# Five more norms summed in rows, and the pooling weights' low part on GpSimd instead of VectorE

## The chip, the cores and the metric

The kernel runs on one core of a Trainium2 chip. Its time is device microseconds of one launch. Five engines run their own instruction streams and meet at semaphores: TensorE (PE in the rows; PEld its weight loads), VectorE (DVE), ScalarE (ACT), GpSimd (POOL) and SyncE (SP), which issues the loads of the weights. Weights and activations come from HBM into SBUF; matmuls write PSUM, eight banks.

## The reference

A prompt of 128 tokens and a latent of 1024 tokens, 1024 channels each, go through two layers. Layer 0 mixes tokens with a gated linear recurrence in both directions, layer 1 with means over windows of 2, 4, 8 and 16 tokens. After each mixer comes a SwiGLU block of width 2816. Every block has an RMS norm ahead of it and one behind it:

```python
def rms_norm(x, g):
    return x * lax.rsqrt(jnp.mean(x * x, axis=-1, keepdims=True) + EPS) * g

def layer_forward(x, cond, p, h0):
    sh1, sc1, g1, sh2, sc2, g2 = modulation(cond, p['mod_w'], p['mod_b'])
    h = rms_norm(x, p['mix_pre_g']) * (1.0 + sc1) + sh1
    y = rglru_mixer(h, ...) if p['kind'] == 'rglru' else pool_mixer(h, ...)
    x = x + g1 * rms_norm(y, p['mix_post_g'])
    h = rms_norm(x, p['ffn_pre_g']) * (1.0 + sc2) + sh2
    gate, up = jnp.split(h @ w_in, 2, axis=-1)
    return x + g2 * rms_norm((silu(gate) * up) @ w_out, p['ffn_post_g'])

def pool_mixer(h, pool_w, pool_b, pool_scale):
    pooled = [centred_window_mean(h_gi, win) - h_gi for gi, win in enumerate((2, 4, 8, 16))]
    return (einsum('btgc,gcd->btgd', pooled, pool_w) + pool_b) * pool_scale
```

## The kernel before, in words

Activations lie channels on partitions, tokens on columns. The 1152 tokens form three column groups (0, 1 and 2) of 384. Every product of float32 operands is made of three matmuls: each operand is split into a high part, rounded to the matmul's format, and a low part, the rest; high by high, low by high and high by low are added up in PSUM (line 1042). In the rows mv and hid are moving operands, w the weights, each with _hi and _lo.

**Weights.** They come in granules of 128x2048 floats (1 MB). SP loads granule q of the stream into one of two raw slots (lines 970 to 1017; line 980 is the load itself) and waits until the low part of granule q-2 is made. ACT makes the high part (`split_hi`, line 1488) into one of three weight slots; the low part, raw minus high, is made by GpSimd in one instruction (`split_lo`, line 2665), by VectorE in one (line 2210), or by VectorE in two halves (`split_lo_half`, line 2217), put between its additions of outs into y (line 2485). Which it is, `HALVES`, `AFTER_POOL`, `ON_DVE` and `ON_POOL` say.

**SwiGLU steps.** A step (layer, s) takes one block of 256 hidden channels for one or more groups: gate and up products, the hidden product on VectorE (line 2462) with its parts by ACT (line 1800) and VectorE (line 2465), then eight outs, m = 0 to 7, added into y by VectorE, or taken by ACT where they are the first (line 1808). Three steps also carry the pooling mixer's products of one group (`POOL_AFTER`): step (0, 17) has group 0's, (1, 1) group 1's, (1, 6) group 2's. Ahead of these, ACT makes the high parts of three granules: the pooling weights, then the next step's gate, then its up. In time the three lie at 1258, 1429 and 1582 us.

**Norms.** Each group has norms numbered in order; in layer 0, norm 1 is the mixer's post norm and norm 2 the SwiGLU's pre norm, both in the stage of the out projection (about 430 to 565 us). ACT squares, GpSimd adds the squares over the eight channel tiles (line 2682), TensorE adds over partitions. It does so in one of two forms. In columns: three 128x1 sums (line 1128, two matmul passes each), VectorE adds epsilon and inverts (lines 2066, 2067), ACT takes the root (line 1518), and TensorE spreads the result over the partitions (line 1139). In rows, for the norms (group, number) listed in `ROWS`: one product with a matrix of ones that leaves the sum on all partitions (line 1117), ACT's root of the whole row (line 1512), and four reciprocals of 128x96 on VectorE (line 2083).

**Order.** Each engine's order is written out when the program is built. `feed_forward_work` lists the steps' work with a place in TensorE's time, `planned` puts the norms' chains into the gaps by estimated costs (`INVERSE` is that of one reciprocal), and `upto` emits what is due. An engine runs its instructions strictly in that order.

Of the kernel before, what the change touches and what calls it, by code (L numbers as in the profile page):

```python
# [104 lines left out]
POOL_AFTER = {(0, SNAKE + 11): 0, (1, 1): 1, (1, 6): 2}  # L105
# [12 lines left out]
def own(layer, s):  # L118

    return own(layer, s - 1) if s and STEPS[layer][s - 1][0] == STEPS[layer][s][0] else s  # L120
# [34 lines left out]
WEIGHT = {item: w for w, item in enumerate(i for i in STREAM if i[0] != "mod")}  # L155
# [156 lines left out]
def norm_cols(g, n):  # L312
    return UNEVEN[g] if n in UNEVEN_NORMS else EVEN[g]
# [71 lines left out]
def places(t):  # L385

    return [t + k / KT * AT_PRODUCT["gate"] for k in PLACES]
# [6 lines left out]
def next_granules(layer, s):  # L394

    if last_own(layer, s) != s:
        return []
    later = [WEIGHT[i] for i in STREAM[Q["down", layer, own(layer, s)] + 1:] if i[0] != "mod"]
    return later[:3 if (layer, s) in POOL_AFTER else 2]


SPLIT_HI, SPLIT_LO, SMALL, TAKE, FOLD = 2.0, 4.6, 0.3, 1.2, 1.0
FIRST_DVE, FIRST_MARGIN, BESIDE_POOL, LATE = 0.5, 1.0, 0.35, 1.0
OP = {"DVE": 0.7, "ACT": 0.6, "POOL": 1.1}
MOD_SUM, COEFS, SUM, ROOT, SPREAD, TURN_Y, LANDING, PE_MARGIN = 7.7, 4.0, 1.5, 1.7, 1.2, 1.2, 9.0, 1.5
INVERSES, INVERSE = 4, 0.6
ROWS = [(0, 3), (0, 4), (0, 5), (0, 7), (1, 1), (1, 3), (1, 4), (1, 5), (1, 6), (1, 7), (2, 3), (2, 4), (2, 5), (2, 6)]


def feed_forward_work():  # L410


    work, hooks = [], []
    for i, n in enumerate(W_OUTS):
        hooks += places(AT_WOUT[i])
        work.append(("ACT", ("take", n), AT["out", n], TAKE))
    for w, t in J1_SPLITS.items():
        low = ("DVE", 2.2) if w in DVE_SPLITS else ("POOL", SPLIT_LO)
        work += [("ACT", ("split", w), t, SPLIT_HI), (low[0], ("split", w), t + SPLIT_HI, low[1])]
    for g, t in ((1, MIXED_T[0]), (2, MIXED_T[1])):  # L420
        for part, (t0, t1) in enumerate(MIXED_PARTS):
            work += [("ACT", ("mixed", g, part), t + part * 1e-3, 0.45 * (t1 - t0)),
                     ("DVE", ("mixed", g, part), t + 0.5 + part * 1e-3, 0.5 * (t1 - t0))]
    for layer in range(2):
        for s in range(len(STEPS[layer])):
            groups = STEPS[layer][s][1]
            t = AT["gate", PAIR[layer, s, groups[0], 0]] - AT_PRODUCT["gate"]
            if own(layer, s) == s:
                w = WEIGHT["down", layer, s]
                t += DOWN_LATER if (layer, s) == (0, 0) else 0.0  # L430
                low = ("DVE", 2.2) if w in LAST_SPLITS else ("POOL", SPLIT_LO)
                work += [("ACT", ("split", w), t, SPLIT_HI), (low[0], ("split", w), t + SPLIT_HI, low[1])]
            if (layer, s) == (0, 1):
                work.append(("DVE", ("mod", -1), AT["gate", PAIR[layer, s, groups[0], 0]] + 0.4, MOD_SUM))
            for g in groups:
                for j in range(HB):
                    k = PAIR[layer, s, g, j]
                    t = AT["up", k]
                    for at in (AT["gate", k] - AT_PRODUCT["gate"], AT["gate", k]):
                        hooks += places(at) if at < FIRST_END or at >= LAST_BEGIN else [at]  # L440
                    one = FIRST_DVE if not FIRST_END <= t < LAST_BEGIN else OP["DVE"]
                    work += [("ACT", ("silu", k), AT["gate", k], OP["ACT"]), ("DVE", ("mul", k), t, one),
                             ("ACT", ("hi", k), t + 0.8, OP["ACT"]), ("DVE", ("lo", k), t + 1.6, one)]
                    if k in SUM_AFTER_PAIR:
                        work.append(("DVE", ("mod", k), t + 2.4, MOD_SUM))
                    if k in (COEFS_AFTER, LAST_COEFS_AFTER):
                        work.append(("DVE", ("coefs", k), t + 2.4, COEFS))
            for w in next_granules(layer, s):
                i = next_granules(layer, s).index(w)
                at = LATE_UP if w in AFTER_POOL else 1.5 + SPLIT_HI * i  # L450
                work.append(("ACT", ("split", w), t + at, SPLIT_HI))
                if w in HALVES:
                    for half, (g, m) in enumerate(HALVES[w]):
                        work.append(("DVE", ("split", w, half), AT["out", OUT[layer, s, g, m]] + 0.75, 1.1))
                elif w in AFTER_POOL:
                    work.append(("DVE", ("split", w), t + at + SPLIT_HI, 2.2))
                else:
                    before = [v for v in next_granules(layer, s)[:i] if v in ON_POOL]
                    at = 9.0 if (layer, s) in POOL_AFTER else 1.5 + SPLIT_HI + SPLIT_LO * len(before)
                    work.append(("POOL", ("split", w), t + at, SPLIT_LO))  # L460
            outs = [(n, True) for g in groups for n in range(OUT[layer, s, g, 0], OUT[layer, s, g, KT - 1] + 1)]
            if (layer, s) in POOL_AFTER:
                outs += [(OUT["pool", POOL_AFTER[layer, s], m], False) for m in range(KT)]
            for i, (n, added) in enumerate(outs):
                if not 0 < i < 4 or AT["out", n] >= LAST_BEGIN:
                    hooks.append(AT["out", n] - AT_PRODUCT["out"])
                if n in FRESH:
                    work.append(("ACT", ("add", n), AT["out", n], OP["ACT"]))
                elif added:
                    work.append(("DVE", ("add", n), AT["out", n], FIRST_DVE if not FIRST_END <= AT["out", n] < LAST_BEGIN else OP["DVE"]))  # L470
    return work, hooks


def planned():
# [31 lines left out]
    def norm(chain, g, squared):  # L506
# [5 lines left out]
        summed = put(("PE", chain, g), added, SUM)  # L512
        if (g, norms[g] - 1) in ROWS:
            t = put(("ACT", chain, g), summed, ROOT)
# [157 lines left out]
def halves():  # L672


    places, late = {}, []
    for layer in range(2):
        for s, (b, groups) in enumerate(STEPS[layer]):
            later = next_granules(layer, s)
            if (layer, s) in POOL_AFTER:
                places[later[0]] = [(groups[-1], 3), (groups[-1], 4)]  # L680
                late.append(later[2])
            elif later and later[0] in LAST_SPLITS:
                for w, g in zip(later, groups):
                    places[w] = [(g, 3), (g, 5)]
            elif later and len(groups) == 1 and (layer, s) != (0, 0):
                places[later[1]] = [(groups[-1], 5), (groups[-1], 7)]
    return places, late
# [8 lines left out]
def program(nc, a, scratch_x, scratch_h, consts, outs):  # L696
    ctx = ExitStack()
    at = [(nc.sbuf_base + 31) // 32 * 32]
# [72 lines left out]
    with ctx:  # L771
# [110 lines left out]
        def ready(w):  # L882

            return (w_lo_dve, ON_DVE.index(w) + 1) if w in ON_DVE else (w_lo_pool, ON_POOL.index(w) + 1)
# [17 lines left out]
        def spread_count(g, n):  # L902
            return sum((g, v) not in ROWS for v in range(n + 1))

        def spread_of(g, n):

            t0, t1 = norm_cols(g, n)
            return bank[norm_bank(g, n)][:, SPREAD_AT:SPREAD_AT + t1 - t0]
# [119 lines left out]
        def _(pe):  # L1028
# [74 lines left out]
            def norm_sum(g):  # L1103
# [11 lines left out]
                t0, t1 = norm_cols(g, n)  # L1115
                if (g, n) in ROWS:
                    pe.matmul(spread_of(g, n), ones[:, :], acc[:, g % 2, 0:t1 - t0], start=True, stop=True  # L1117
# [247 lines left out]
            def norm_turns(g):  # L1365

                yield
                norm_sum(g)
                if (g, sums[g] - 1) not in ROWS:
                    yield  # L1370
# [82 lines left out]
        def _(act):  # L1453
# [53 lines left out]
            def norm_root(g):  # L1507
                n = stats[g]
                t0, t1 = norm_cols(g, n)
                if (g, n) in ROWS:  # L1510
                    act.wait_ge(sum_ready[g], n + 1)
# [490 lines left out]
        def _(dve):  # L2002
# [67 lines left out]
            def norm_inverse(g, n):  # L2070

                if (g, n) not in ROWS:
                    yield
# [578 lines left out]
        def _(pool):  # L2652
# [46 lines left out]
            z, s, s2, t = lam[:, 1, :], lam[:, 3, :], lam[:, 4, :], lam[:, 5, :]  # L2699
# [35 lines left out]
            def ffn_step(layer, s, upto):  # L2735
                for w in ([WEIGHT["down", layer, s]] if own(layer, s) == s else []) + next_granules(layer, s):
                    if w in ON_POOL:
                        upto(DUE["POOL", "split", w])
                        if (layer, s) in POOL_AFTER and w != WEIGHT["down", layer, s]:
                            pool.wait_ge(*ready(WEIGHT["pool", POOL_AFTER[layer, s]]))  # L2740
                        split_lo(w)

            def first_norms(g):
# [141 lines left out]
```

## Time and profile before

| | us |
|---|---|
| median of 3 runs | 2267.19 (2266.12 to 2271.28) |
| profiled execution | 2266.86 |
| its span | 2265.1 |
| TensorE busy | 2231.6 (99%) |
| VectorE busy | 1374.7 (61%) |
| ACT busy | 884.2 (39%) |
| GpSimd busy | 713.9 (32%) |

TensorE is busy nearly throughout, at a mean granted clock of 0.997 of full speed. The other engines' idle time costs nothing in itself; what counts is where TensorE waits. A row of the timeline gives start, duration, engine, line, what is written from what, and in brackets how long the engine had been idle and who released it.

### The profile page before, as it was taken

The page shows a single profiled execution, that of the slowest core. Times are in us where ns is not written, and L with a number is a line of the kernel's source. Part 1 is how long each engine was busy: PE and PEld are TensorE (multiplying, and loading weights), DVE is VectorE, ACT ScalarE, POOL GpSimd, SP SyncE. Part 2 cuts the span into 40 slices and gives each one's busy share as a digit, 9 for nine tenths or more (in the row PEclk, how much of TensorE's full clock was granted, in tenths as well). Part 3 has the DMA queues.
Part 4 walks back from the last instruction along what each step waited for, and adds up shares of the span by engine and source line. Part 5 has one row for each costly group of instructions (what it writes and reads, how often), then busy time and mean ns, then how long its engine had stood idle before and what let it go on. Part 6 is the DMA issues. An engine that isn't in the chain of part 4 may idle for free.

```text
span 2265.1 us, 31519 instructions
## 1 busy us (share of the span) xinstructions
PE 2231.6 (99%) x12816; PEld 2174.0 (96%) x12816; DVE 1374.7 (61%) x2288; ACT 884.2 (39%) x1226; POOL 713.9 (32%) x310
## 2 busy tenths in 40 slices
PE   8999999999999999999999999999999999999998
PEld 4988899999999999999999998999999999999998
DVE  6589855768757656533476687888365244443246
ACT  4587863344111111232353545654443323111134
POOL 3500021542121021332553545542353334121232
PEclk9999999999999999999999999999999999999999
DMA  9323233341433233433343454352343143321323
GB/s 306 120 76 106 96 129 138 127 152 63 134 109 125 94 98 112 132 129 103 112 140 122 150 171 136 130 198 80 124 155 131 56 135 126 112 75 56 102 94 121
DMA packets 211697, 276.12 MB, mean 122 GB/s; under 512 B 4776, under 2 KB 194784, under 8 KB 211040
## 3 DMA queue, kind: packets, MB, share of 16 engines
q1 hardware_dynamic: 183056, 224.36, 30.1%
q10 hardware_dynamic: 26768, 40.30, 5.1%
q0 software_dynamic: 1728, 9.44, 1.0%
q8 instruction: 101, 1.65, 0.3%
q14 instruction: 44, 0.36, 0.0%
HBM read 245.76 MB, written 28.32 MB: 121 GB/s over the span
## 4 chain that ended last, share of the span: by engine, by line
PE 85%; DVE 6%; issue 3%; ACT 2%; POOL 2%; DMA 1%; SPq 0%; ACTq 0%; POOLq 0%; DVEq 0%
PE bank L1042 82%; PE bank L1072 1%; DVE y L2142 1%; PE bank L1097 1%; POOL acc L2682 1%; POOL w_lo L2665 1%; ACT w_hi L1488 1%; DMA mod_stage<-in_l_mod_w 0%; DMA raw<-in_l_ffn_w_out 0%; DVE hid_lo L2465 0%; DVE pool_sum L2551 0%; DVE w_lo L2217 0%; PE bank L1117 0%; DVE y L2127 0%; DVE y L2485 0%
## 5 line engine op out<-in xcount | busy, mean ns | idle before, releaser
L1042 PE MATMUL bank<-mv_hi,w_hi 128*128 128x384 f32 (+2 forms) x2736 | 925.4, 338 | 7.6 <-ACT y L1808 4.1
L1042 PE MATMUL bank<-mv_lo,w_hi 128*128 128x384 f32 (+2 forms) x2736 | 918.4, 336 | 0.0
L1042 PE MATMUL bank<-mv_hi,w_lo 128*128 128x384 f32 (+2 forms) x2736 | 918.2, 336 | 0.0
L2665 POOL TENSOR_TENSOR w_lo<-raw,w_hi 128x2048 fp32r<-128x2048 f32 x106 | 491.4, 4641 | 1167.3 <-ACT w_hi L1488 1099.6
L1042 PEld LDWEIGHTS bank<-mv_hi,w_hi 128*128 128x128 f32 x2736 | 515.2, 188 | 14.0 <-issue 8.7
L1042 PEld LDWEIGHTS bank<-mv_lo,w_hi 128*128 128x128 f32 x2736 | 515.3, 188 | 0.8
L1042 PEld LDWEIGHTS bank<-mv_hi,w_lo 128*128 128x128 f32 x2736 | 515.1, 188 | 0.0
L1488 ACT ACTIVATE w_hi<-raw 128x2048 fp32r<-128x2048 f32 x159 | 299.6, 1908 | 393.1 <-DMA raw<-in_l_ffn_w_out 219.5
L1042 PE MATMUL bank<-hid_hi,w_hi 128*128 128x384 f32 (+2 forms) x1056 | 361.5, 342 | 6.4 <-DVE hid_lo L2465 3.1
L2485 DVE TENSOR_TENSOR y<-y,bank 128x384 f32<-128x384 f32 (+2 forms) x480 | 258.6, 553 | 160.3 <-PE bank L1042 160.3
L1042 PE MATMUL bank<-hid_hi,w_lo 128*128 128x384 f32 (+2 forms) x1056 | 355.7, 337 | 0.0
L1042 PE MATMUL bank<-hid_lo,w_hi 128*128 128x384 f32 (+2 forms) x1056 | 355.5, 337 | 0.0
L2462 DVE TENSOR_TENSOR hid<-hid,bank 128x384 f32<-128x384 f32 (+2 forms) x132 | 72.9, 552 | 446.6 <-PE bank L1042 446.4
L1800 ACT ACTIVATE hid_hi<-hid 128x384 fp32r<-128x384 f32 (+2 forms) x132 | 69.3, 525 | 413.9 <-DVE hid L2462 413.4
L1042 PEld LDWEIGHTS bank<-hid_hi,w_hi 128*128 128x128 f32 x1056 | 198.4, 188 | 14.2 <-DVE hid_lo L2465 5.2
L1042 PEld LDWEIGHTS bank<-hid_lo,w_hi 128*128 128x128 f32 x1056 | 198.5, 188 | 1.1
L1042 PEld LDWEIGHTS bank<-hid_hi,w_lo 128*128 128x128 f32 x1056 | 198.4, 188 | 0.0
L2039 DVE SCALAR_TENSOR_TENSOR mod_sum_norms<-raw,cond,mod_sum_norms 128x256 f32<-128x256 f32 x420 | 168.8, 479 | 0.0
L1793 ACT ACTIVATE hid<-bank 128x384 f32<-128x384 f32 (+2 forms) x132 | 64.4, 488 | 247.8 <-PE bank L1042 247.3
L2682 POOL TENSOR_TENSOR acc<-acc,wide 128x384 f32<-128x384 f32 (+2 forms) x124 | 138.3, 1115 | 20.8 <-ACT wide L1498 13.1
L2465 DVE TENSOR_TENSOR hid_lo<-hid,hid_hi 128x384 fp32r<-128x384 f32 (+2 forms) x132 | 102.3, 775 | 68.7 <-ACT hid_hi L1800 68.3
L2217 DVE TENSOR_TENSOR w_lo<-raw,w_hi 128x1024 fp32r<-128x1024 f32 x72 | 109.0, 1515 | 3.0 <-ACT w_hi L1488 2.8
(163 smaller groups left out, 1831.5 us busy)
## 6 DMA issues: line engine op xcount, KB each, us to landing
raw<-in_l_ffn_w_in SPq DMA_DIRECT2D x92, 1024.0 KB, 5.1
raw<-in_l_ffn_w_out SPq DMA_DIRECT2D x46, 1024.0 KB, 4.9
raw<-in_l_mod_w SPq DMA_DIRECT2D x42, 1024.0 KB, 5.1
residual<-y ACTq DMA_DIRECT2D x10, 1536.0 KB, 6.9
x_old<-residual ACTq DMA_DIRECT2D x10, 1536.0 KB, 7.0
raw<-in_l_w_in SPq DMA_DIRECT2D x8, 1024.0 KB, 5.5
mod_stage<-in_l_mod_w SPq DMA_DIRECT2D x6, 1024.0 KB, 12.3
raw<-in_l_w_out SPq DMA_DIRECT2D x6, 1024.0 KB, 5.4
```

The source lines that it names most:

```text
L1042: last = pe.matmul(out, w, x, start=start and n == 0, stop=stop and n == len(steps) - 1)
L1072: last = pe.matmul(out, cond[:, k, :], src[:, k * 2 * P:(k + 1) * 2 * P], start=k == 0, stop=k == KT - 1)
L1488: act.activation(w_hi[:, slot(w), :], raw[:, q % 2, :], ACT.Copy).then_inc(w_hi_ready, 1)
L1793: act.activation(h, bank[2 * (k % 2)][:, 0:t1 - t0], ACT.Silu).then_inc(silu_done, 1)
L1800: act.activation(hid_hi[:, j, t0:t1], h, ACT.Copy).then_inc(hid_hi_done, 1)
L2039: ins = dve.scalar_tensor_tensor(out=dst, in0=src_k, scalar=cond[:, k, c:c + 1], in1=dst, op0=ALU.mult, op1=ALU.add)
L2217: ins = dve.tensor_tensor(w_lo[:, slot(w), v], raw[:, q % 2, v], w_hi[:, slot(w), v].bitcast(F32), ALU.subtract)
L2462: dve.tensor_tensor(h, h, bank[2 * (k % 2) + 1][:, 0:t1 - t0], ALU.mult).then_inc(hid_ready, 1)
L2465: dve.tensor_tensor(hid_lo[:, j, t0:t1], h, hid_hi[:, j, t0:t1].bitcast(F32), ALU.subtract).then_inc(hid_split, 1)
L2485: dve.tensor_tensor(dst, dst, src, ALU.add).then_inc(out_taken, 1)
L2665: pool.tensor_tensor(w_lo[:, slot(w), :], raw[:, q % 2, :], w_hi[:, slot(w), :].bitcast(F32), ALU.subtract).then_inc(w_lo_pool, 1)
L2682: ins = pool.tensor_tensor(out, tiles[:, tile[0]] if m == 1 else out, tiles[:, tile[1]], ALU.add)
```

## The change

Five norms join `ROWS`: post and pre norm of group 0 in layer 0, the pre norm of group 1, and both of group 2. The planner's cost of one reciprocal goes from 0.6 to 0.5. In the three steps with pooling products the pooling weights' low part is made by GpSimd as soon as its high part is there, and the gate's by VectorE in halves behind the additions of outs 3 and 4; before it was the other way round, and GpSimd waited for VectorE's halves of the pooling weights (the two lines that go at the end).

```diff
-INVERSES, INVERSE = 4, 0.6
-ROWS = [(0, 3), (0, 4), (0, 5), (0, 7), (1, 1), (1, 3), (1, 4), (1, 5), (1, 6), (1, 7), (2, 3), (2, 4), (2, 5), (2, 6)]
+INVERSES, INVERSE = 4, 0.5
+ROWS = [(0, 1), (0, 2), (0, 3), (0, 4), (0, 5), (0, 7), (1, 1), (1, 2), (1, 3), (1, 4), (1, 5), (1, 6), (1, 7), (2, 1), (2, 2), (2, 3), (2, 4), (2, 5), (2, 6)]
...
-                    at = 9.0 if (layer, s) in POOL_AFTER else 1.5 + SPLIT_HI + SPLIT_LO * len(before)
+                    at = 1.5 + SPLIT_HI + SPLIT_LO * len(before)
...
             if (layer, s) in POOL_AFTER:
-                places[later[0]] = [(groups[-1], 3), (groups[-1], 4)]
+                places[later[1]] = [(groups[-1], 3), (groups[-1], 4)]
...
                         upto(DUE["POOL", "split", w])
-                        if (layer, s) in POOL_AFTER and w != WEIGHT["down", layer, s]:
-                            pool.wait_ge(*ready(WEIGHT["pool", POOL_AFTER[layer, s]]))
                         split_lo(w)
```

In the three pooling steps the rows of VectorE and GpSimd read alike before and after, since the granules have the same names: only which granule an instruction works on has changed, and when GpSimd may start. The places where rows move:

TensorE's order near the sums of (1, 2) and (2, 1), 501 to 508 us; bank7 holds group 1's norm, bank6 group 2's. Before:

```order
L1042 MATMUL bank0<-mv_hi_53,w_lo_52 128x384
L1139 MATMUL bank7<-const_85,var_92 128x128 x3
L1128 MATMUL bank6<-ones_86,acc_84 128x1 x3
L1042 MATMUL bank1<-mv_hi_53,w_hi_50 128x384
L1042 MATMUL bank1<-mv_lo_54,w_hi_50 128x384
```

After:

```order
L1042 MATMUL bank0<-mv_hi_53,w_lo_52 128x384
L1117 MATMUL bank6<-acc_84,ones_86 128x384
L1042 MATMUL bank1<-mv_hi_53,w_hi_50 128x384
L1042 MATMUL bank1<-mv_lo_54,w_hi_50 128x384
L1042 MATMUL bank1<-mv_hi_53,w_lo_52 128x384
```

The spread of (1, 2) is gone and the sum of (2, 1) stands at the same product in its new form.

VectorE's order from the norms (1, 2) and (2, 1) into the first SwiGLU step, before:

```order
L2066 TENSOR_SCALAR var<-bank 128x3
L2067 RECIPROCAL var<-var 128x3
L2066 TENSOR_SCALAR var<-bank 128x3
L2067 RECIPROCAL var<-var 128x3
L2192 SCALAR_TENSOR_TENSOR wide<-y,coef,bank 128x384 x4
L2462 TENSOR_TENSOR hid<-hid,bank 128x384
L2179 SCALAR_TENSOR_TENSOR mv_lo<-wide,modv,mv_hi 128x384
L2192 SCALAR_TENSOR_TENSOR wide<-y,coef,bank 128x384
L2465 TENSOR_TENSOR hid_lo<-hid,hid_hi 128x384
```

After:

```order
L2083 RECIPROCAL bank<-acc 128x96 x4
L2192 SCALAR_TENSOR_TENSOR wide<-y,coef,bank 128x384 x4
L2083 RECIPROCAL bank<-acc 128x96
L2462 TENSOR_TENSOR hid<-hid,bank 128x384
L2083 RECIPROCAL bank<-acc 128x96 x2
L2465 TENSOR_TENSOR hid_lo<-hid,hid_hi 128x384
L2083 RECIPROCAL bank<-acc 128x96
L2179 SCALAR_TENSOR_TENSOR mv_lo<-wide,modv,mv_hi 128x384
```

Four reciprocals of (1, 2) come ahead of its pre norm, and the four of (2, 1) lie around the first hidden product's two instructions, ahead of the low parts of the pre norm.

VectorE's order in the step at 1318 us, between the second norm's pieces and the hidden product, the difference:

```order
-L2083 RECIPROCAL bank<-acc 128x96 x2
+L2083 RECIPROCAL bank<-acc 128x96
+L2164 TENSOR_TENSOR wide<-y,bank 128x384
 L2462 TENSOR_TENSOR hid<-hid,bank 128x376
 L2465 TENSOR_TENSOR hid_lo<-hid,hid_hi 128x376
```

One reciprocal has gone ahead to an earlier place, and a piece of the next norm (line 2164) now stands ahead of the hidden product; on ACT three pieces of the pooling source (lines 1860 and 1866) have come ahead of that product's high part.

## Rows read from the trace of the kernel before

**Rows 1.** The page's chain that ended last, by engine
```profile
PE 85%; DVE 6%; issue 3%; ACT 2%; POOL 2%; DMA 1%; SPq 0%; ACTq 0%; POOLq 0%; DVEq 0%
```

**Rows 2.** Timeline of TensorE: start us, us, engine line op out<-in xcount
```profile
432.31 0.72 PE L1128 MATMUL bank<-ones,acc 128*128 128x1 f32 x6
432.89 0.42 PE L1042 MATMUL bank<-mv_hi,w_hi 128*128 128x384 f32 x1
...
438.19 0.83 PE L1139 MATMUL bank<-const,var 128*128 128x128 f32 x6
438.77 0.42 PE L1042 MATMUL bank<-mv_hi,w_hi 128*128 128x384 f32 x1
...
472.05 0.81 PE L1117 MATMUL bank<-acc,ones 128*128 128x384 f32 x2
472.87 0.34 PE L1042 MATMUL bank<-mv_lo,w_hi 128*128 128x384 f32 x1
```

**Rows 3.** Timeline of TensorE, waits for sums of squares; [idle before <-releaser]
```profile
456.53 0.83 PE L1128 MATMUL bank<-ones,acc 128*128 128x1 f32 x6 [1.88 <-POOL acc L2682]
...
501.09 0.83 PE L1128 MATMUL bank<-ones,acc 128*128 128x1 f32 x6 [1.19 <-POOL acc L2682]
...
541.42 0.72 PE L1128 MATMUL bank<-ones,acc 128*128 128x1 f32 x5 [0.38 <-POOL acc L2682]
```

**Rows 4.** Timeline of VectorE ahead of group 0's post norm
```profile
439.35 2.29 DVE L2210 TENSOR_TENSOR w_lo<-raw,w_hi 128x2048 fp32r<-128x2048 f32 x1 [5.83 <-ACT w_hi L1488]
```

**Rows 5.** Windows: stretch, us, busy by engine, PEclk, DMA share, GB/s
```profile
457.50:461.20 3.70, 3.70 (x14) 3.70 (x13) 0.23 (x2) 0.20 (x1) 2.01 (x2) 0.54 0.77 277
502.20:505.60 3.40, 3.40 (x13) 3.40 (x12) 0.13 (x1) 0.00 (x0) 0.88 (x1) 0.51 0.52 182
1604.87:1608.06 3.19, 3.19 (x11) 3.19 (x11) 0.87 (x2) 2.09 (x4) 1.00 (x1) 0.51 0.48 155
```

**Rows 6.** Timelines of ACT, VectorE, GpSimd and TensorE, first pooling step
```profile
1258.93 3.70 ACT L1488 ACTIVATE w_hi<-raw 128x2048 fp32r<-128x2048 f32 x2
1262.51 1.22 DVE L2217 TENSOR_TENSOR w_lo<-raw,w_hi 128x1024 fp32r<-128x1024 f32 x1
1265.39 4.60 POOL L2665 TENSOR_TENSOR w_lo<-raw,w_hi 128x2048 fp32r<-128x2048 f32 x1 [16.02 <-DVE w_lo L2217]
1264.23 0.44 PE L1042 MATMUL bank<-hid_hi,w_hi 128*128 128x376 f32 x1 [0.15 <-DVE y L2485]
```

**Rows 7.** Timelines of ACT, GpSimd and VectorE, a half beside GpSimd
```profile
1402.72 1.91 ACT L1488 ACTIVATE w_hi<-raw 128x2048 fp32r<-128x2048 f32 x1
1404.71 4.56 POOL L2665 TENSOR_TENSOR w_lo<-raw,w_hi 128x2048 fp32r<-128x2048 f32 x1 [6.92 <-ACT w_hi L1488]
1407.29 3.06 DVE L2217 TENSOR_TENSOR w_lo<-raw,w_hi 128x1024 fp32r<-128x1024 f32 x1 [2.60 <-ACT w_hi L1488]
```

**Rows 8.** Timelines of ACT and TensorE, second pooling step
```profile
1429.44 3.71 ACT L1488 ACTIVATE w_hi<-raw 128x2048 fp32r<-128x2048 f32 x2
1434.77 0.44 PE L1042 MATMUL bank<-hid_hi,w_hi 128*128 128x384 f32 x1 [0.17 <-DVE y L2485]
```

**Rows 9.** Timelines of ACT, SP and TensorE, third pooling step
```profile
1582.86 3.71 ACT L1488 ACTIVATE w_hi<-raw 128x2048 fp32r<-128x2048 f32 x2
1595.86 0.37 SPq L980 DMA_DIRECT2D raw<-in_l_ffn_w_in  x1
1601.04 1.91 ACT L1488 ACTIVATE w_hi<-raw 128x2048 fp32r<-128x2048 f32 x1 [3.21 <-DMA raw<-in_l_ffn_w_in]
1603.47 0.41 PE L1042 MATMUL bank<-mv_hi,w_hi 128*128 128x384 f32 x1 [4.07 <-ACT y L1808]
```

**Rows 10.** Timelines of VectorE and TensorE near 1318; ACT's group by form
```profile
1317.61 1.36 DVE L2083 RECIPROCAL bank<-acc 128x96 f32<-128x96 f32 x2
1320.60 0.44 PE L1042 MATMUL bank<-hid_hi,w_hi 128*128 128x376 f32 x1 [0.20 <-DVE hid_lo L2465]
...
L1860 ACT ACTIVATE pool_src<-wide,modv,coef 128x384 f32<-128x384 f32 x8 | 5.6, 697 | 0.0
```

## The prediction

> **What bounds the kernel now.** I read the page first: its chain that ended last lies on TensorE for 85% of the span, with VectorE, ACT and GpSimd taking single per cents [rows 1]. So only two things can move the time: what TensorE issues, and what makes it wait. Then I read TensorE's timeline for gaps around every place that the change touches, and the timelines of VectorE, ACT and GpSimd at the same places, to see who ends last there. A product of 128x384 is issued every 0.17 us; a gap above that is a wait, and the bracket at a row's end names its releaser. Last I read the windows after the longest gaps for the granted clock.
>
> **The sum's base.** The profiled execution took 2266.86 us, 1.76 over its span and 0.33 under the median of the three runs shown, so what I add to it stands for the median within about that much.
>
> **Five norms in rows.** Each of the five drops six column matmuls and six spreading matmuls and gets one row product of two passes. The column sums take 0.58 us until the next product starts (432.31 to 432.89) and the spread the same (438.19 to 438.77); each delays the product behind it by another 0.09 or so (it is 0.26 to the next instead of 0.17), 1.34 together. A row sum puts the second product behind it 0.82 later, 0.17 of it that product's own, so 0.65 [rows 2]. Saved: 0.69 a norm, 3.4 for five, if nothing else ends last.
>
> But three of these sums stand where TensorE waits for GpSimd's sum of squares: 1.88 us, 1.19 us and 0.38 us [rows 3]. There, arriving earlier only lengthens the wait.
> - Norm (0,1): VectorE's post norm stands behind a low part of 2.29 us that itself waits for ACT, and starts at 441.56 in either form [rows 4]. The squares of (0,2) follow it, so the wait of 1.88 grows by the 0.69 saved ahead of it. Gain 0.
> - (0,2), (1,2) and the spread of (2,1): the chain of group 1 starts at its own row sum, which TensorE reaches 0.7 earlier, so the wait of 1.19 stays near 1.1. Some 2.4 us are in hand when TensorE nears the sum of (2,2).
> - (2,1) and (2,2): four reciprocals at about 0.68 us (two took 1.36 [rows 10]) take the place of two instructions on 128x3 on VectorE, up to 2.7 us more in each chain. (2,1)'s stand between a hidden product's two instructions and ahead of the post norm, whose squares GpSimd adds for (2,2). I work out GpSimd's sum ready at about 540.7 instead of 541.3, so TensorE, 2.4 us earlier, waits 2.2 us instead of 0.38, and only 0.6 is left. Behind it, (2,2)'s reciprocals alternate with the copies out of PSUM, and what its dropped spread saves goes into waiting for VectorE.
>
> So I take -0.6 for the stage of rows. From below: all 3.4 stay. From above: +0.9, if (2,2)'s 2.7 us of reciprocals end last in place of the spread's 0.67 and an estimated 0.5 for the two small instructions with their handover: 1.5 lost, 0.6 of it in hand. The wait of 1.19 is followed by a stretch at clock 0.51, as the wait of 1.88 is by one at 0.54 [rows 5]: half speed, 1.2 instead of 2.4 GHz, in which ten products came every 0.32 us, 1.47 us lost. Shortened to 1.1, the one at 501 may lose its drop; I count half of that, -0.7.
>
> **The pooling weights' low part on GpSimd.** In the two steps at 1258 and 1429 us ACT makes the high parts of the pooling weights and then of the gate; VectorE makes the pooling low part in two halves behind the additions of outs 3 and 4; GpSimd starts on the gate afterwards [rows 6]. Now GpSimd starts as soon as the first high part is there. In the row pair of 1402.72 and 1404.71 that is 2.0 us after ACT's start, so here at 1260.9, and it ends 4.6 later at 1265.5. VectorE's first half of the gate comes up at 1262.5, inside that.
>
> What happens then is on record. At 1407.29 a half beside GpSimd's low part of 1404.71 to 1409.27 took 3.06 us, not 1.22, and ended 1.08 after GpSimd [rows 7]. Every other half in the timeline that comes up during such an instruction ends as late behind it. So the first half ends at 1266.6 instead of 1263.7. Behind it in VectorE's order wait the addition of out 4, the second half, and the addition of out 5; TensorE's out 6 and out 7 reuse these banks and already wait 0.15 us for VectorE [rows 6], so there is no cover. Cost: +2.9 us. The step at 1429 is the same pattern 170.5 us later (1429.44 against 1258.93), and TensorE's wait of 0.17 there leaves no cover either [rows 8]: +2.9.
>
> The Trainium skill, page "SBUF — State Buffer", section "Who interferes with whom", speaks against the change: VectorE and GpSimd share one port pair as an exclusive lock, a VectorE operation with two SBUF inputs contends with a GpSimd operation that reads SBUF, and whoever starts first holds it for its whole instruction. By that rule the half would start only at GpSimd's end and take its full 1.22, +3.0 instead of +2.9; the trace has it a little shorter, at 1.08. The rule leaves the order open, which is the third rival below.
>
> Waits of 3 us are longer than those two that ended in half clock [rows 5], so I add 1.47 to each: +2.9 together, bounded by 0 and 2.9.
>
> In the third step (1582 us) nothing of this holds. Its outs are taken by ACT, and VectorE's halves run at 1593, after GpSimd would be done (1582.86 + 2.0 + 4.6 = 1589.5). SP's load of the up weights waits for the pooling low part: 1595.86 now, 1589.5 then. ACT's high part of up waits 3.21 us for that load, at 1601.04, with ACT's take of out 7 behind it, and TensorE loses 4.07 us to that [rows 9]. With the load 6.3 us earlier ACT waits only for the weight slot, which comes free with out 7 at about 1598.4. TensorE goes on 2.6 us earlier (ACT's 1601.04 becomes 1598.4), 1.5 of the wait stay, and without the long wait the half clock behind it (0.51 from 1604.87 to 1608.06 [rows 5]) should go: -2.6 - 1.47 = -4.1. Bounds: -2.6, and -5.5 if all 4.07 go. Loads behind it only move earlier; SP waits for nothing new.
>
> **The planner's 0.5.** It only moves instructions between the norms' pieces. At 1318 us VectorE's shift (L2164) comes ahead of the hidden product, and ACT's three pieces of the pooling source ahead of its high part; these take 0.7 us for the large one [rows 10] and about 1.0 in all. TensorE already waits 0.20 us for that hidden product, so +0.9; near 1401 the opposite exchange may save 0.3. Together +0.6, bounds 0 and +1.2.
>
> Sum: -0.6 - 0.7 + 2.9 + 2.9 + 2.9 - 4.1 + 0.6 = +3.9, so 2266.9 + 3.9 = 2270.8 us.
>
> **Rivals.**
> 1. Slower by more: half clock also follows the 2.2 us wait at 541 (+1.47), stays at 501 (+0.7) and stays in the third step (+1.47). +7.5, 2274.4 us. For it: a wait of 1.19 us was enough once. Against: not every wait of that size in the trace was followed by it. It decides from the second of these drops on.
> 2. The 3 us are given back. Between the two steps TensorE waits several times for VectorE and ACT; if those chains don't shift with TensorE, up to 3 us vanish there: 2268 us. Against: their work begins with the same additions that are held up.
> 3. The block doesn't come, because VectorE's half starts before GpSimd gets going or ACT's high parts are late: both steps cost 0, and with -0.6 - 0.7 + 0.6 - 4.1 the time is 2262.1 us; with all 3.4 of TensorE's saving kept as well it is 2259.3. Against: GpSimd has idled some 16 us ahead of its gate part at 1265.39 [rows 6], and 1.6 us lie between its start and VectorE's.
>
> **How the numbers follow.** Forecast 0.5, rival 1 0.2, rival 2 0.2, rival 3 0.1. About 0.2% (4.5 us) is what a measurement of this kernel tells from no change, so slower begins at 2271.7 and faster below 2262.7. The forecast lies just under the first edge and puts about two fifths of its chance beyond it: 0.2 + 0.2 from rival 1 = 0.40 slower. Rival 3 gives 0.06 of faster and a little comes from terms below their values: 0.07. The rest, 0.53, is within. The range takes the forecast's terms with both clock terms and the stage of rows at their bounds, most of rivals 1 and 2: 2265.5 to 2275.
>
> **What would show it.** Right: a half of the gate of over 3 us on VectorE at about 1262 and 1433, beside GpSimd's low part; TensorE waits of about 3 us for VectorE's addition in both steps, with half clock behind them; the wait at 1599 down from 4.07 to about 1.5; TensorE's wait for GpSimd's sum near 541 above 2 us. Wrong: halves of 1.2 us in those steps; products that keep the 2 us or more in hand beyond 542; no half clock behind waits of 3 us.

## The result and the profile after

The changed kernel takes 2272.36 us in the median of 15 runs (2271.11 to 2275.96), the kernel before 2267.6 us in 15 (2266.12 to 2271.28) beside it: a ratio of 1.0022, 95% interval 1.0016 to 1.0029, or +4.8 us. 2270.8 was predicted, 2265.5 to 2275. The profiled execution took 2274.49 us, 2.1 above that median, with a span of 2272.4.

The chain that ended last still lies on TensorE; ACT has gone from 2% to 3%, DMA from 1% to 2% [rows 1]:

```profile
PE 85%; DVE 6%; ACT 3%; issue 2%; POOL 2%; DMA 2%; SPq 0%; ACTq 0%; DVEq 0%; POOLq 0%
```

I laid the 11,952 products of line 1042 in the two profiled executions side by side in order; the table has how much later each place comes than before, and the step of that difference.

| place (us after) | step | later than before, behind it |
|---|---|---|
| start, to 57 | +0.96 | +0.96 |
| stage of rows, to 551 | -1.65 | -0.69 |
| small steps, to 1184 | -0.7 | -1.4 |
| 1184: wait of 1.88, half clock | +2.04, +1.53 | +2.2 |
| 1269: first pooling step, half clock | +2.86, +1.1 | +6.2 |
| 1326: a wait of 0.20 gone | -0.45 | +5.7 |
| 1389: half clock; 1408: a wait of 0.48 gone | +1.3, -0.76 | +6.2 |
| 1437 and 1444: second pooling step, half clock | +0.35, +2.84, +0.94 | +10.3 |
| 1611: third pooling step, half clock gone | -2.60, -1.57 | +6.1 |
| 1715: wait of 1.01 | +1.17 | +7.3 |

The profiled execution after lies 2.1 over its median and the one before 0.7 under its own, so about 4.8 of the 7.3 is what the medians show. The start's 0.96 differs from run to run.

The three waits for GpSimd's sum in the stage of rows, on TensorE's timeline (start us, us, engine line operation, [idle before <-releaser]); they answer to [rows 3]:

```profile
457.84 1.65 PE L1117 MATMUL bank<-acc,ones 128*128 128x384 f32 x2 [3.01 <-POOL acc L2682]
...
501.31 0.91 PE L1117 MATMUL bank<-acc,ones 128*128 128x384 f32 x2 [0.90 <-POOL acc L2682]
...
540.67 0.91 PE L1117 MATMUL bank<-acc,ones 128*128 128x384 f32 x2 [2.42 <-POOL acc L2682]
```

1.88 has become 3.01, 1.19 has become 0.90, and 0.38 has become 2.42: most of what TensorE no longer does it now waits for.

The first pooling step after the change, timelines of ACT, GpSimd, VectorE and TensorE, in that order, against [rows 6]:

```profile
1261.11 3.71 ACT L1488 ACTIVATE w_hi<-raw 128x2048 fp32r<-128x2048 f32 x2
...
1263.09 4.59 POOL L2665 TENSOR_TENSOR w_lo<-raw,w_hi 128x2048 fp32r<-128x2048 f32 x1 [11.53 <-ACT w_hi L1488]
...
1264.85 3.92 DVE L2217 TENSOR_TENSOR w_lo<-raw,w_hi 128x1024 fp32r<-128x1024 f32 x1
1268.69 0.53 DVE L2485 TENSOR_TENSOR y<-y,bank 128x376 f32<-128x376 f32 x1
1269.15 1.21 DVE L2217 TENSOR_TENSOR w_lo<-raw,w_hi 128x1024 fp32r<-128x1024 f32 x1
...
1269.28 0.44 PE L1042 MATMUL bank<-hid_hi,w_hi 128*128 128x376 f32 x1 [3.01 <-DVE y L2485]
```

GpSimd starts 1.98 behind ACT's start and ends at 1267.68; VectorE's first half comes up 1.76 later, takes 3.92 and ends at 1268.77, 1.09 behind GpSimd. Out 4's addition follows, and TensorE has waited 3.01 for it. The second half, with GpSimd done, takes 1.21. The second step is the same (answers to [rows 8]; GpSimd, VectorE, TensorE):

```profile
1437.96 4.59 POOL L2665 TENSOR_TENSOR w_lo<-raw,w_hi 128x2048 fp32r<-128x2048 f32 x1 [10.65 <-ACT w_hi L1488]
...
1439.72 3.91 DVE L2217 TENSOR_TENSOR w_lo<-raw,w_hi 128x1024 fp32r<-128x1024 f32 x1
...
1444.15 0.69 PE L1042 MATMUL bank<-hid_hi,w_hi 128*128 128x384 f32 x1 [3.00 <-DVE y L2485]
```

In the third, the load of up (SP), ACT's high part of it and TensorE's wait, against [rows 9]:

```profile
1599.79 0.37 SPq L980 DMA_DIRECT2D raw<-in_l_ffn_w_in  x1
...
1608.72 1.91 ACT L1488 ACTIVATE w_hi<-raw 128x2048 fp32r<-128x2048 f32 x1 [0.61 <-PE bank L1042]
...
1611.16 0.41 PE L1042 MATMUL bank<-mv_hi,w_hi 128*128 128x384 f32 x1 [1.47 <-ACT y L1808]
```

The load was issued at 1595.86 and TensorE was 10.3 later here, so it comes 6.4 earlier in the work. ACT waits for the slot that out 7's products free (0.61 <-PE) instead of 3.21 for the load, and TensorE 1.47 instead of 4.07.

Windows behind five of these waits (stretch, its length, busy us of PE, PEld, DVE, ACT and POOL, granted clock, DMA share, GB/s), against [rows 5]:

```profile
457.84:461.50 3.66, 3.66 (x11) 3.05 (x12) 1.37 (x3) 0.58 (x1) 2.89 (x3) 0.57 1.03 371
...
1184.50:1188.00 3.50, 3.50 (x11) 3.50 (x12) 1.42 (x3) 3.50 (x4) 2.27 (x1) 0.52 0.00 0
1269.30:1273.00 3.70, 3.70 (x13) 3.33 (x14) 2.06 (x3) 0.00 (x0) 0.00 (x0) 0.59 1.05 353
...
1444.20:1447.50 3.30, 3.30 (x11) 3.30 (x12) 2.05 (x3) 0.00 (x0) 0.00 (x0) 0.51 1.04 347
1611.20:1614.40 3.20, 3.20 (x19) 3.20 (x20) 2.23 (x2) 2.72 (x6) 0.35 (x1) 1.00 0.06 16
```

Half clock, 1.2 instead of 2.4 GHz, behind the first four; none behind 1611, where there was some before.

The wait at 1184 was not in the prediction. Followed back, timelines of ACT and TensorE after:

```profile
1168.96 1.92 ACT L1488 ACTIVATE w_hi<-raw 128x2048 fp32r<-128x2048 f32 x1 [7.91 <-DMA raw<-in_l_ffn_w_out]
...
1184.49 0.60 PE L1042 MATMUL bank<-hid_hi,w_hi 128*128 128x384 f32 x1 [1.88 <-DVE hid_lo L2465]
```

and ACT before:

```profile
1168.30 1.92 ACT L1488 ACTIVATE w_hi<-raw 128x2048 fp32r<-128x2048 f32 x1 [5.84 <-DMA raw<-in_l_ffn_w_out]
```

TensorE is 1.4 earlier than before, but ACT gets the down weights 0.66 later, and hands that on through the pooling source's pieces and VectorE's sums to the hidden product, where TensorE waits 1.88. The load's landing time says more: DMA by queue from 1162 to 1172, after (packets, MB, share; then the issues with KB and us to landing):

```profile
q8 instruction: 1, 0.02, 0.6%
q14 instruction: 1, 0.01, 0.2%
...
raw<-in_l_ffn_w_out SPq DMA_DIRECT2D x1, 1024.0 KB, 6.8
```

and before, from 1163 to 1172, with no packet of either instruction queue:

```profile
raw<-in_l_ffn_w_out SPq DMA_DIRECT2D x1, 1024.0 KB, 4.7
```

Two instruction fetches, one packet on each of the two queues, fall into the load now, and it takes 6.8 instead of 4.7. Experiments 5, 10 and 11 test whether they are the cause.

### The profile page after: what moved, and what is told of

Read it like the earlier page. It is cut to its first block, busy times and chain, and to the rows that moved or that the text cites. A ratio compares the mean times of both kernels' runs of the same rounds, so it can differ in the third digit from the quotient of the medians.

```text
span 2272.4 us, 31425 instructions
## 1 busy us (share of the span) xinstructions
PE 2232.5 (98%) x12766; PEld 2173.6 (96%) x12766; DVE 1390.4 (61%) x2298; ACT 886.2 (39%) x1226; POOL 712.8 (31%) x310
## 4 chain that ended last, share of the span: by engine, by line
PE 85%; DVE 6%; ACT 3%; issue 2%; POOL 2%; DMA 2%; SPq 0%; ACTq 0%; DVEq 0%; POOLq 0%
PE bank L1042 81%; DVE y L2142 1%; PE bank L1072 1%; PE bank L1097 1%; ACT w_hi L1488 1%; DMA raw<-in_l_ffn_w_out 1%; POOL w_lo L2665 1%; POOL acc L2682 1%; PE bank L1117 1%; DVE mv_lo L2179 0%; DVE y L2127 0%; DVE hid_lo L2465 0%; DVE y L2480 0%; DVE pool_sum L2551 0%; DVE hid L2462 0%
## 5 line engine op out<-in xcount | busy, mean ns | idle before, releaser
L2217 DVE TENSOR_TENSOR w_lo<-raw,w_hi 128x1024 fp32r<-128x1024 f32 x72 | 114.0, 1584 | 3.3 <-ACT w_hi L1488 3.1
```

Source lines behind the costliest of these rows:

```text
L2217: ins = dve.tensor_tensor(w_lo[:, slot(w), v], raw[:, q % 2, v], w_hi[:, slot(w), v].bitcast(F32), ALU.subtract)
```

## The experiments

Times are medians; the kernel before took 2268.58 us beside the first four (27 runs), 2267.79 beside the next four (26), 2268.36 beside 9 to 11 (12) and 2267.7 beside 12 (14).

**1. The exchange alone.** The norms and `INVERSE` as before, GpSimd and VectorE exchanged in all three steps; the edit is against the changed kernel, lists shortened.

```diff
-INVERSES, INVERSE = 4, 0.5
-ROWS = [(0, 1), (0, 2), (0, 3), ... (2, 1), (2, 2), (2, 3), ...]
+INVERSES, INVERSE = 4, 0.6
+ROWS = [(0, 3), (0, 4), (0, 5), (0, 7), (1, 1), (1, 3), ...]
```

> The pooling weights' low part on GpSimd and the gate's halves on VectorE in all three steps; the five norms and the planner's cost as before. Theory A (GpSimd's instruction blocks VectorE's half): +2.9 us in each of the steps at 1258 and 1429 with about 0.9 of half clock behind each, -4.1 in the third: about +3.6 us, 2271.2. Theory B (the five norms cost the time, the exchange is free): -4.1 us from the third step alone, 2263.5.

Measured 2271.32 us, ratio 1.0012 [1.0003, 1.0021], +2.7. Waits of 3.02 at 1267.66, 3.00 at 1442.41 and 1.48 at 1609.48, as in the changed kernel: the exchange by itself costs two blocks and gains the third step.

**2. The exchange in the third step alone**; the edit is against 1, and `(0, SNAKE + 11)` is step (0, 17).

```diff
+SWAP_NOT = [(0, SNAKE + 11), (1, 1)]
-                at = 1.5 + SPLIT_HI + SPLIT_LO * len(before)
+                at = 9.0 if (layer, s) in SWAP_NOT else 1.5 + SPLIT_HI + SPLIT_LO * len(before)
-                places[later[1]] = [(groups[-1], 3), (groups[-1], 4)]
+                places[later[0 if (layer, s) in SWAP_NOT else 1]] = [(groups[-1], 3), (groups[-1], 4)]
+                if (layer, s) in SWAP_NOT and w != WEIGHT["down", layer, s]:
+                    pool.wait_ge(*ready(WEIGHT["pool", POOL_AFTER[layer, s]]))
```

> The exchange in the third step alone, the first two as before. A and B alike: TensorE's wait near 1599 falls from 4.07 to about 1.5 us and its half clock goes, -4.1 us: 2263.5. If the gain needs something that the other steps do, or is given back before the end: no change, 2267.6.

2262.85 us, ratio 0.9974 [0.9964, 0.9984], -5.7; TensorE's wait at 1601.40 is 1.48, and the half clock behind it is gone. The third step is a gain, and the other two are the loss: 8.5 us lie between 1 and 2.

**3. Norms and `INVERSE` alone**, without the exchange: the first diff's two lines the other way round, put into the kernel before.

> The five norms in rows and the planner's 0.5, the exchange undone in all three steps. A: TensorE waits more for GpSimd's sums at 455 and 540, and the stage nets -1.6 us, with up to +1.2 from the order near 1385: between -1.6 and 0, about 2267. B: the norms carry what the change lost and what the third step gained: about +8 us, 2275.

2269.26 us, ratio 1.0004 [0.9995, 1.0014]: no difference. After a start 1.7 later TensorE gains 3.2 in the stage of rows and goes on 1.5 ahead of before. Most of that is clock: none of the waits there is followed by half clock in this execution, where before has two such stretches, 1.47 each by the prediction's count, so little of it is the norms' own. A wait of 1.40 at 1183.41, one of 0.56 at 1707.76 and a longer half clock at 1603 take it back. The down load took 6.3 there with both fetches inside.

**4. The whole change, the gate's halves later**: behind outs 6 and 7 in the first two steps.

```diff
-                        if (g, m) in HALVES.get(w, []):
-                            half = HALVES[w].index((g, m))
+                        if (at := (g, m - 3 if (layer, s) in ((0, SNAKE + 11), (1, 1)) else m)) in HALVES.get(w, []):
+                            half = HALVES[w].index(at)
```

> The whole change, with the gate's two halves in the steps at 1258 and 1429 put behind the additions of outs 6 and 7 instead of 3 and 4, so that GpSimd is done when they come up. A: halves of 1.22 us, no wait of 3 us in either step: change's +4.8 less 2 x 3.9, about -3 us, 2264.5. B: the halves are as slow or the waits move to another addition: 2271 to 2272.

2263.48 us, ratio 0.9974 [0.9964, 0.9984]. GpSimd and VectorE in the first step:

```profile
1262.18 4.65 POOL L2665 TENSOR_TENSOR w_lo<-raw,w_hi 128x2048 fp32r<-128x2048 f32 x1 [11.53 <-ACT w_hi L1488]
...
1266.90 1.22 DVE L2217 TENSOR_TENSOR w_lo<-raw,w_hi 128x1024 fp32r<-128x1024 f32 x1
```

GpSimd ends at 1266.83, the half starts at 1266.90 and takes 1.22; neither 3 us wait is left. The same instructions in the same amount, moved by a few us, are worth 8.9 us by the medians (2272.36 against 2263.48, not measured beside each other) and 9.9 by each one's difference from the kernel before beside it (+4.8 and -5.1). The change's waits at 1184 and 1715 stand here too, 1.27 at 1185 and 0.51 at 1704.

**5. Experiment 3 with 25 one-column matmuls at the start**, where TensorE waits for its first loads; they shift where the instruction fetches fall.

```diff
+            for _ in range(N):
+                pe.matmul(bank[NORM_BANK][:, 508:509], ones[:, :], ones[:, 0:1], start=True, stop=True)
             pe.wait_ge(const_landed, 16)
```

with N = 15, and 10 ahead of `pe.wait_ge(cond_ready, 1)`.

> The five norms in rows with the exchange undone, as before in this study, and 25 matmuls of one column (ones by ones, into a PSUM column that nobody reads) added where TensorE waits in the first 19 us: as many TensorE instructions as the five norms took away. Theory C (the shorter TensorE program shifts its instruction fetches into two loads of down weights): the loads at about 1161 and 1687 us land after 4.8 to 5.0 us instead of 6.3, TensorE's waits of 1.40 near 1183 and 0.56 near 1707 go, about -2 us against the same kernel without them, 2267. Rival D (the loads are late because of VectorE's or ACT's order, or by chance): landing 6 us or more, the waits stay, 2269 or above.

2268.12 us, ratio 1.0001 [0.9992, 1.001]. The waits at 1183 and 1707 are gone. From 1163 to 1172:

```profile
q14 instruction: 1, 0.01, 0.2%
...
raw<-in_l_ffn_w_out SPq DMA_DIRECT2D x1, 1024.0 KB, 4.8
```

One fetch inside, and the load lands in 4.8. The time didn't follow: half clock behind the waits at 458 and 541, which 3 has behind neither (2.9 together in the stage of rows), and a wait of 0.63 at 1321.95 took the place. So the fetches explain the wait at 1183, but not by themselves why five norms in rows show no gain.

**6. The kernel before with 39 such matmuls** (22 and 17 at the two places), to bring both fetches into its load.

> The kernel before with 39 such matmuls (156 TensorE instructions) in the first 19 us; with about 256 instructions to a fetch this puts its fetches where the rows kernels have them. C: the load at about 1163 us lands after 6 us or more instead of 4.7, and TensorE waits over 1 us near 1183 where it did not: 2269 to 2271 with what the added matmuls cost at the start. D: the load lands after 4.8 us and nothing new is waited for: 2268 to 2269.

2272.68 us, ratio 1.0024 [1.0015, 1.0034]; but the start alone cost 6.9 there, and one fetch fell into the load (5.0), so no wait came at 1184. A miss: it doesn't test what it was made for.

**7. The third step and three norms in rows**, (0, 1), (0, 2) and (1, 2), with `INVERSE` 0.5; without (2, 1) and (2, 2), whose wait at 541 gives their saving back.

> The exchange in the third step alone, the planner's 0.5, and three of the five norms in rows: (0,1), (0,2) and (1,2); (2,1) and (2,2) stay in columns. If (2,1)'s reciprocals are what makes the sum of (2,2) late, TensorE's wait near 540 falls from 2.4 to below 1.5 us and the stage keeps about 2 us instead of 1.6. Theory A with C: -4.1 and -2, less what a shifted fetch costs: 2261 to 2263. If GpSimd's part of the chain is as late without the reciprocals, the wait stays above 2 us, and the time is that of the third step alone, 2263.

2264.36 us, ratio 0.9983 [0.9975, 0.9992]. The wait at 541 is back at 0.36 and the stage keeps 3.1, with one stretch of half clock fewer than before; the load took 6.7 with both fetches inside, and TensorE waits 1.73 at 1182.41 and 0.94 at 1542.57. The three norms show no gain on top of the third step: -3.4 against -5.7 in 2, with intervals that overlap.

**8. GpSimd's pooling low part cut into two instructions of 128x1024** in the first two steps, the rest as in the change; one run, whose time tells little.

```diff
+                cuts = (0, GC // 2, GC) if w in (WEIGHT["pool", 0], WEIGHT["pool", 1]) else (0, GC)
+                for a, b in zip(cuts, cuts[1:]):
...
```

> The whole change with GpSimd's pooling low part cut into two instructions of 128x1024 in the steps at 1258 and 1429. If VectorE's half waits for the one instruction of GpSimd that runs: the first half ends about 1.1 us behind GpSimd's first piece or within 2 us of its start, and TensorE's first wait of 3.0 us falls to about 1 (0.7 + 0.15), though the second half may meet the second piece and make out 7 wait instead. If VectorE is late for another reason (its inputs, ACT): the wait stays 3 us.

2269.93 us. GpSimd, VectorE and TensorE in the first step:

```profile
1260.82 5.73 POOL L2667 TENSOR_TENSOR w_lo<-raw,w_hi 128x1024 fp32r<-128x1024 f32 x2 [11.53 <-ACT w_hi L1488]
...
1262.57 1.74 DVE L2217 TENSOR_TENSOR w_lo<-raw,w_hi 128x1024 fp32r<-128x1024 f32 x1
1264.24 0.53 DVE L2485 TENSOR_TENSOR y<-y,bank 128x376 f32<-128x376 f32 x1
1264.69 2.93 DVE L2217 TENSOR_TENSOR w_lo<-raw,w_hi 128x1024 fp32r<-128x1024 f32 x1
...
1264.83 0.44 PE L1042 MATMUL bank<-hid_hi,w_hi 128*128 128x376 f32 x1 [0.83 <-DVE y L2485]
1268.13 0.44 PE L1042 MATMUL bank<-hid_hi,w_hi 128*128 128x376 f32 x1 [2.00 <-DVE y L2485]
```

VectorE's first half is let in at GpSimd's seam and ends at 1264.31, while GpSimd goes on to 1266.55; the second half meets the second instruction and ends 1.07 behind it. A half waits for one running GpSimd instruction, not for GpSimd's work; cut in two, one wait of 3.0 becomes 0.83 and 2.00. The Trainium skill, page "SBUF — State Buffer", section "Who interferes with whom", has it so: a VectorE instruction with two SBUF inputs contends with a GpSimd instruction that reads SBUF, and whoever issues first keeps the shared ports for its whole instruction. The trace agrees, but for the blocked half's end, 1.07 to 1.09 us behind GpSimd's where its own duration is 1.22.

**9. The exchange in all three steps with the late halves**, without the norms (1 with the edit of 4).

> The exchange in all three steps with the gate's halves of the first two behind outs 6 and 7; norms and planner's cost as before. Theory A: nothing is blocked, the third step gains 4.1, and TensorE's small waits of 0.15 to 0.29 us in the first two steps go too: -4.1 to -5.5, 2262.5 to 2264, as good as the third step alone. If late halves delay the next step's gate: above 2264.

2260.92 us, ratio 0.9969 [0.9957, 0.998], -7.4. In the profiled execution the first two steps gain about 0.5 each, once nothing blocks; by the times it can't be told from 2.

**10. Experiment 7 with 15 one-column matmuls** at the start.

> Third step's exchange, three norms in rows, the planner's 0.5, and 15 one-column matmuls at the start, as many TensorE instructions as the three norms took away. Theory C: both fetches no longer fall into the load near 1160 together, TensorE's wait of 1.73 us near 1183 goes, and the stage's 3 us stay: 2 to 3 us less than without the 15, about 2261.5, the fastest so far. D: the wait stays, 2264.

2260.92 us, ratio 0.9966 [0.9954, 0.9979], 3.4 under 7, not measured beside it; the wait at 1182 is gone. A new one shows what the prediction had feared at 1318. VectorE, ACT and TensorE there:

```profile
1316.71 0.54 DVE L2464 TENSOR_TENSOR hid<-hid,bank 128x376 f32<-128x376 f32 x1
...
1316.89 0.40 ACT L1862 ACTIVATE pool_halo<-wide,modv,coef 128x16 f32<-128x16 f32 x1 [0.80 <-DVE wide L2166]
1317.20 0.20 ACT L1868 ACTIVATE pool_src<-pool_halo 128x16 f32<-128x16 f32 x1
1317.31 0.69 ACT L1862 ACTIVATE pool_src<-wide,modv,coef 128x384 f32<-128x384 f32 x1
1317.90 0.50 ACT L1802 ACTIVATE hid_hi<-hid 128x376 fp32r<-128x376 f32 x1
...
1319.04 0.44 PE L1042 MATMUL bank<-hid_hi,w_hi 128*128 128x376 f32 x1 [1.38 <-DVE hid_lo L2467]
```

The hidden product is there at 1317.25, ACT does three pieces of the pooling source first, and TensorE waits 1.38, where it waited 0.20 before.

**11. Experiment 4 with 25 one-column matmuls.**

> The change with late halves, and 25 one-column matmuls in the first 19 us. C: the waits of 1.27 near 1183 and 0.51 near 1707 go, about -1.5 against the same without them, 2261.5 to 2262.5. D: as without them, 2263.5.

2261.25 us, ratio 0.9968 [0.9957, 0.9979], 2.2 under 4, but with intervals that overlap. The waits at 1185 and 1704 are gone; the wait of 2.42 at 541 stays, with half clock behind it.

**12. All gains together**: 10 with the exchange in every step and late halves in the first two.

> The three gains put together: the exchange in all three steps with VectorE's gate halves behind GpSimd's long instructions, three of the five norms in rows with INVERSE at 0.5, and fifteen one-column matmuls at the start. Theory A (the gains lie in different stages and add): the exchange with late halves gave -7.4 us alone, the three rows with the padding about -2 to -3 us on top of the third step; the sum is about -9 to -10 us, 2258 to 2260 us. Theory B (a gain in one stage is eaten by a wait in the next, as with the five norms): no lower than the exchange alone, 2261 us; a wait on VectorE's low parts near 1319 or on a load near 1184 or 1707 shows where it went.

2261.63 us, ratio 0.9975 [0.9965, 0.9984]. Theory A falls: no lower than 9. Its wait at 1318.69 is 1.39, the one of 10, and experiment 9 has none there; what decides over it stands below, under the planner's 0.5.

Experiments 9, 10, 11 and 12 are 6.1 to 7.4 us under the kernel before; they can't be told from each other, and 9 is the smallest edit of them.

## Why the prediction was right

**The two blocks** are as foreseen to a tenth: the half over 3 us, its end 1.08 behind GpSimd (1.09 measured), +2.9 in each step (+2.86 and +2.84). Experiments 1, 2 and 4 show them as the cause and experiment 8 shows by what. Half clock followed both, but cost 1.1 and 0.9, not 1.47 each: TensorE's next wait for VectorE in each step, 0.29 and 0.28 before, was gone behind it.

**The third step** gave -2.60 and -1.57 against -2.6 and -1.47, by the way that was foreseen: load 6.4 earlier, ACT held by the slot, 1.5 of the wait left.

**The stage of rows.** The wait near 541 was to be 2.2 and is 2.42; the one at 501 lost its half clock; the stage gave -1.65 against -1.3. That this is so near is luck: the forecast counted half of the clock's 1.47 and all of it came, so the norms themselves gave about -0.2 of the -0.6. Not as foreseen was the wait at 457, 3.01 where 1.88 + 0.69 = 2.57 stood, with half clock behind it as before.

**The planner's 0.5** was the step that failed in the changed kernel: +0.9 near 1318 did not come, and the wait of 0.20 there went. The order was read rightly, its slack wrongly, and the slack hangs on the same block. VectorE and GpSimd, before and then after:

```profile
1307.29 5.10 DVE L2142 SCALAR_TENSOR_TENSOR y<-y,coef,x_old 128x128 f32<-128x128 f32 x2
...
1307.46 4.66 POOL L2665 TENSOR_TENSOR w_lo<-raw,w_hi 128x2048 fp32r<-128x2048 f32 x1 [6.77 <-ACT w_hi L1488]
...
1313.45 0.74 DVE L2142 SCALAR_TENSOR_TENSOR y<-y,coef,x_old 128x128 f32<-128x128 f32 x2
...
1314.10 4.62 POOL L2665 TENSOR_TENSOR w_lo<-raw,w_hi 128x2048 fp32r<-128x2048 f32 x1 [7.25 <-ACT w_hi L1488]
```

The second of VectorE's two instructions in each row, on 128x256, came 0.09 behind GpSimd's start before and took 4.84; after, it came 0.39 ahead and took 0.48. So VectorE is early after, and waits for TensorE ahead of the hidden product:

```profile
1324.61 0.55 DVE L2462 TENSOR_TENSOR hid<-hid,bank 128x376 f32<-128x376 f32 x1 [1.98 <-PE bank L1042]
```

That instruction was caught, 0.02 to 0.09 behind GpSimd's start, in five of the fourteen profiled executions. TensorE then waited 0.20 or less with 0.6 (before and 2), and 0.63 to 1.39 with 0.5 (5, 10 and 12). In the nine others it didn't wait there with either cost. So +0.9 is the size of a caught execution, and the changed kernel's wasn't one. The -0.3 near 1401 was no work of the planner's either: the wait of 0.48 went (-0.76) behind a stretch of half clock at 1389, as it did in 1, 2 and 9, which have 0.6.

**Left out** was the load near 1163: +3.6 with its half clock, in a place that the change doesn't touch. "Loads behind it only move earlier" looked at the order of the loads, not at what shares the DMA engines with them. In experiment 3 the same wait takes back 1.6 of what the stage of rows gained. Left out too were the later start (+0.96), half clock at 1389 less the wait at 1408 (+0.5), and the waits at 1437 (+0.35) and, behind a second slow load near 1690, 1715 (+1.17). The other two misses (1.35 at 1318, 0.9 of clock in the two steps) partly cancel them, so the total is closer than its terms, by luck. Of the 1.6 by which the forecast is low, 0.7 is its base: the profiled execution before lies that far under the median of 15.

**Rivals.** Rival 3, in which the block doesn't come, is ruled out by 1; experiment 4 is what it would look like. Rival 2 is ruled out: between the two steps only the waits of 0.20 at 1326 and 0.48 at 1408 went, and both went in 2 as well, which has no block. Rival 1's half clock behind the wait at 541 came in 4, 5 and 11 but not in the profiled execution after, and the drops at 501 and in the third step did not stay; what the other runs of the changed kernel had there, no trace shows.

## What to carry to other kernels

A VectorE operation with two operands in SBUF that comes up while GpSimd makes a low part ends behind it, in the trace before 1.08 us for a half of 128x1024 and 0.41 for the 128x384 operation of line 2465: place it by when GpSimd ends, as in experiment 4, and price it by the wait of whoever needs the VectorE work queued behind. A start 0.1 us earlier or later can decide it, as at 1307. Work taken from the engine that bounds the kernel is worth little or nothing where the next thing it does is wait for another (1.88 to 3.01, 0.38 to 2.42); look for the releaser of the next wait first. A change that alters the number of instructions can slow a load hundreds of microseconds away, so compare the kernels product by product along the whole span before crediting a gain to the place that was edited.

## What the runs showed of the hardware

**Instruction fetches and loads.** The 1 MB load near 1163 landed in 4.7 to 5.1 us with no instruction packet inside or with one (before, experiments 1, 2, 5, 6, 9 to 12) and in 6.1 to 6.8 with a packet on both q8 and q14 (after, 3, 4, 7, 8). Experiments 5, 10 and 11 moved the fetches by 15 to 25 matmuls and the wait went with them. It doesn't always take both: the down load issued between 1680 and 1694 landed in 5.8 to 6.4 with one q8 packet about 1 us behind its issue (after, 3, 4, 6, 8) and in 4.7 to 5.2 in the nine executions without one; TensorE waits 0.42 to 1.01 behind it, at 1704 to 1715, in those five alone. Near 1163, in 6, a q8 packet 4.4 us behind the issue left it at 5.0; what makes the difference is open.

**Half clock is not decided by the wait's length.** The same wait of 3.0 us for GpSimd's sum, TensorE in experiments 3 and 5:

```profile
458.51 0.91 PE L1117 MATMUL bank<-acc,ones 128*128 128x384 f32 x2 [3.01 <-POOL acc L2682]
```

```profile
457.88 0.91 PE L1117 MATMUL bank<-acc,ones 128*128 128x384 f32 x2 [3.02 <-POOL acc L2686]
```

and the window of 458.0 to 461.5 behind it, 3 and then 5:

```profile
458.00:461.50 3.50, 2.99 (x15) 2.73 (x16) 1.43 (x3) 0.85 (x2) 3.34 (x4) 1.00 1.02 368
```

```profile
458.00:461.50 3.50, 3.50 (x13) 3.23 (x14) 2.06 (x4) 0.58 (x1) 2.78 (x3) 0.65 1.03 372
```

Full clock in one, 0.65 in the other. In experiment 9 a wait of 1.87 there left the clock at 1.00, where before 1.88 was followed by 0.54 [rows 5]. A wait of 1.86 to 1.89 near 1385 stands in all fourteen profiled executions; ten have half clock behind it, four (before, 3, 5 and 12) none. Each such stretch is worth 0.9 to 1.6 us, as much as the smaller terms of the sum, and which of them a run gets I couldn't predict.
